# The inversion of the gated-DeltaNet blocks: 16x16 blocks by row substitution on VectorE, with the blocks copied to the lanes through DRAM, in place of three levels of block doubling on TensorE

## The reference

```python
kb = kc * bc[..., None]
a = jnp.where(strict, jnp.einsum('nbhid,nbhjd->nbhij', kb, kc) * decay, 0.0)
ia = a + jnp.eye(lc, dtype=jnp.float32)
u = lax.linalg.triangular_solve(ia, vc * bc[..., None], left_side=True, lower=True, unit_diagonal=True)
w = lax.linalg.triangular_solve(ia, kb * jnp.exp(gcum)[..., None], left_side=True, lower=True, unit_diagonal=True)
```

## Time and profile before

| what | us |
|---|---|
| median of 3 runs | 1892.87 |
| lowest, highest | 1892.07, 1893.97 |
| profiled execution, span | 1893.0 |
| PE busy | 1867.0 |
| DVE busy | 1087.0 |
| ACT busy | 729.3 |
| POOL busy | 223.4 |

### The profile page before, as it was taken

How to read it: one execution, slowest core, us unless ns; L and a number is a source line. 1 busy time by engine, 2 the same in 40 slices (tenths; PEclk the granted TensorE clock), 3 DMA queues, 4 the chain that set the end, 5 groups by cost and what they waited for, 6 DMA issues and landing times.

```text
span 1893.0 us, 31005 instructions
## 1 busy us (share of the span) xinstructions
PE 1867.0 (99%) x9409; PEld 1579.4 (83%) x9409; DVE 1087.0 (57%) x2433; ACT 729.3 (39%) x1467; POOL 223.4 (12%) x379
## 2 busy tenths in 40 slices
PE   7999999999999999999999999999999999999997
PEld 6999998888888888888888888888888888888886
DVE  6666666888888874564545454433334444444455
ACT  4444444545444433353333333333333333333330
POOL 2343432222222200001110110000000000000000
PEclk9999999999999999999999999999999999999999
DMA  8666665444444435346555646544444555456541
GB/s 216 168 166 162 161 171 126 109 113 111 114 110 113 116 120 161 94 128 163 157 158 161 172 122 170 162 129 128 129 130 142 150 161 161 127 166 211 162 134 67
DMA packets 317412, 270.76 MB, mean 143 GB/s; under 512 B 96600, under 2 KB 230624, under 8 KB 316704
## 3 DMA queue, kind: packets, MB, share of 16 engines
q1 hardware_dynamic: 306880, 250.90, 47.3%
q0 software_dynamic: 10464, 18.99, 4.1%
HBM read 249.73 MB, written 20.06 MB: 143 GB/s over the span
## 4 chain that ended last, share of the span: by engine, by line
PE 98%; DVE 1%; DMA 0%; issue 0%; SPq 0%; ACT 0%; DVEq 0%; POOL 0%; ACTq 0%; POOLq 0%
PE bank L296 71%; PE bank L2013 9%; PE bank L1749 7%; PE bank L1865 2%; PE bank L1242 1%; PE bank L1224 1%; PE bank L1236 1%; PE bank L1218 1%; PE bank L415 0%; DMA x_res<-in_x_sample 0%; PE bank L638 0%; PE bank L1192 0%; PE bank L1285 0%; PE bank L1214 0%; PE bank L1200 0%
## 5 line engine op out<-in xcount | busy, mean ns | idle before, releaser
L272 DVE TENSOR_TENSOR w_lo<-raw,w_hi 128x512 fp32r<-128x512 f32 (+2 forms) x828 | 562.4, 688 | 620.9 <-ACT w_hi L267 616.8
L267 ACT ACTIVATE w_hi<-raw 128x512 fp32r<-128x512 f32 (+2 forms) x828 | 502.4, 616 | 838.6 <-PE bank L296 703.1
L296 PE MATMUL bank<-w_hi,aT_hi 128*128 128x512 f32 (+2 forms) x1776 | 696.3, 392 | 1.7 <-DVE aT_lo L430 1.6
L296 PE MATMUL bank<-w_hi,aT_lo 128*128 128x512 f32 (+2 forms) x1776 | 673.6, 379 | 0.0
L296 PE MATMUL bank<-w_lo,aT_hi 128*128 128x512 f32 (+2 forms) x1776 | 672.6, 379 | 0.0
L296 PEld LDWEIGHTS bank<-w_hi,aT_hi 128*128 128x128 f32 x1776 | 334.8, 189 | 58.7 <-issue 9.7
L296 PEld LDWEIGHTS bank<-w_hi,aT_lo 128*128 128x128 f32 x1776 | 334.0, 188 | 55.7
L296 PEld LDWEIGHTS bank<-w_lo,aT_hi 128*128 128x128 f32 x1776 | 335.1, 189 | 47.7
L296 PE MATMUL bank<-w_hi,hT_hi 128*128 128x512 f32 x288 | 112.1, 389 | 0.0
L296 PE MATMUL bank<-w_lo,hT_hi 128*128 128x512 f32 x288 | 112.1, 389 | 0.0
L296 PE MATMUL bank<-w_hi,hT_lo 128*128 128x512 f32 x288 | 112.0, 389 | 0.0
(11 more groups left out here) (365 smaller groups left out, 1962.5 us busy)
## 6 DMA issues: line engine op xcount, KB each, us to landing
raw<-in_ffn_w_gate SPq DMA_DIRECT2D x176, 256.0 KB, 2.7
raw<-in_ffn_w_up SPq DMA_DIRECT2D x176, 256.0 KB, 2.7
raw<-in_ffn_w_down SPq DMA_DIRECT2D x176, 256.0 KB, 3.4
raw<-in_w_in SPq DMA_DIRECT2D x128, 192.0 KB, 2.4
raw<-in_w_in SPq DMA_DIRECT2D x128, 128.0 KB, 2.3
raw<-in_w_in SPq DMA_DIRECT2D x256, 64.0 KB, 2.3
raw<-in_w_out SPq DMA_DIRECT2D x61, 256.0 KB, 3.3
h_blocks<-sg SPq DMA_DIRECT2D x11, 768.0 KB, 4.6
```

What stands on the lines that cost most here:

```text
L267: nc.scalar.activation(w_hi[:, g % RING, 0:width], raw[:, g % RAW, 0:width], ACT.Copy).then_inc(sem("w_high"), 1)
L272: nc.vector.tensor_tensor(w_lo[:, g % RING, 0:width], raw[:, g % RAW, 0:width], w_hi[:, g % RING, 0:width], ALU.subtract).then_inc(sem("w_ ...
L296: last = nc.tensor.matmul(acc[t][:, 0:width], l[:, k0 + n, t * P:(t + 1) * P], r[:, g % RING, 0:width], start=(n == 0 and j == 0), stop=(n ...
```

## The change

Levels 1, 2 and 3 go from PE and DVE. The inverse of each 16x16 block on the diagonal is computed instead by DVE, one row of the block in each lane (partition): from k = 15 down to 1, column k of the inverse so far times row k of the block is subtracted. For that, each lane needs the whole 16x16 block of its own group of 16 lanes, for all three tiles (768 numbers, 3 KB). SP moves them: 8 stores (one for each group, 16 lanes x 3 tiles x 16 numbers, pieces of 64 bytes) to DRAM, a wait until all have landed, and 8 loads, each of one DRAM row of 3 KB to 16 lanes, into the storage of U and Z, which are one tile now. The move stands in SP's order ahead of load 15 (`LOW_AT`), behind load 14. The row steps are in DVE's slots 19, 22 and 25 (`ROWS_AT`), 5 values of k in each, 2 operations for a k, each followed by `after`. Then T is made from the blocks by a mask, and U from it by transposes as before. Levels 4, 5, 6 move from slots 27, 31, 34 to 28, 32, 35. The value's convolution moves to slots 9 (tap 0) and 14 (taps 1, 2), the rough root to slot 17. The masks of the levels 0 to 3 go from the constants, two smaller ones come.

```diff
+ROWS_AT = (19, 22, 25)
+ROWS_OF = (range(BLOCK - 1, 10, -1), range(10, 5, -1), range(5, 0, -1))
+LOW_AT = NP_IN - 1
+LEVEL_AT = {4: 28, 5: 32, 6: 35}
...
+                A = early[:, 0:TOK].rearrange("p (t c) -> p t c", t=TT)
+                inv, prod = (early[:, TOK + n * TT * BLOCK:TOK + (n + 1) * TT * BLOCK]
+                             .rearrange("p (t c) -> p t c", t=TT) for n in range(2))
...
+                UZ = sb(ctx, "UZ", [P, 2, TT, P])
+                U, Z = UZ[:, 0], UZ[:, 1]
+                low = UZ[:].rearrange("p a t c -> p (a t c)")
+                below = low.rearrange("p (t k c) -> p t k c", t=TT, k=BLOCK)
+                low_blocks = nc.dram_tensor("low_blocks", (GROUPS, TT * BLOCK * BLOCK), F32, kind="Internal").ap()
...
-                    for n in range(1, LEVELS):
+                    for n in range(LOW, LEVELS):
+                        step = n - LOW + 1
                         yield LEVEL_AT[n]
...
-                    after(ins)
-                    after(V.tensor_tensor(B, A, lv[0].unsqueeze(1).broadcast_to([P, TT, P]), ALU.mult))
-                    V.tensor_tensor(T[:], ident.unsqueeze(1).broadcast_to([P, TT, P]), B, ALU.subtract)\
-                        .then_inc(sem("g_T1"), 1)
+                    ins.then_inc(sem("g_A"), 1)
+                    V.tensor_copy(inv, cn[:, C_OWN:C_OWN + BLOCK].unsqueeze(1).broadcast_to([P, TT, BLOCK]))
+                    conv(2, range(1))
+                    yield 14
+                    conv(2, range(1, TAP - 1))
+                    yield 17
+                    rsqrt_rough(nrs[:], nss[:, 1, :], npol[:], after)
+                    for at, ks in zip(ROWS_AT, ROWS_OF):
+                        yield at
+                        dve.wait_ge(sem("g_low_in"), 16 * GROUPS * (h + 1))
+                        for k in ks:
+                            after(V.tensor_tensor(prod[:, :, 0:k], below[:, :, k, 0:k],
+                                                  inv[:, :, k:k + 1].broadcast_to([P, TT, k]), ALU.mult))
+                            after(V.tensor_tensor(inv[:, :, 0:k], inv[:, :, 0:k], prod[:, :, 0:k], ALU.subtract))
+                    V.tensor_tensor(T[:].rearrange("p t (g c) -> p t g c", g=GROUPS),
+                                    inv.unsqueeze(2).broadcast_to([P, TT, GROUPS, BLOCK]),
+                                    cn[:, C_SAME:C_SAME + P].rearrange("p (g c) -> p g c", g=GROUPS).unsqueeze(1)
+                                    .broadcast_to([P, TT, GROUPS, BLOCK]), ALU.mult).then_inc(sem("g_T1"), 1)
                     W("g_T1")
                     V.transpose(U[:, 0, :], T[:, 0, :]).then_inc(sem("g_Ua"), 1)
                     V.transpose(U[:, 1:3, :], T[:, 1:3, :]).then_inc(sem("g_Ub"), 1)
...
-                        if n in (1, 2, 3):
-                            conv(2, range(n - 1, n))
-                        if n == 3:
-                            rsqrt_rough(nrs[:], nss[:, 1, :], npol[:], after)
...
+                def move_low(eng, h):
+
+                    eng.wait_ge(sem("g_A"), h + 1)
+                    for g in range(GROUPS):
+                        own = slice(g * BLOCK, (g + 1) * BLOCK)
+                        eng.dma_start(low_blocks[g].rearrange("(t k c) -> k t c", t=TT, k=BLOCK), A[own, :, own])\
+                            .then_inc(sem("g_low_out"), 16)
+                    eng.wait_ge(sem("g_low_out"), 16 * GROUPS * (h + 1))
+                    for g in range(GROUPS):
+                        eng.dma_start(low[g * BLOCK:(g + 1) * BLOCK, :], low_blocks[g].partition_broadcast(BLOCK))\
+                            .then_inc(sem("g_low_in"), 16)
...
                         for n in range(NP_IN):
                             next_state(sp, n, i)
+                            if n == LOW_AT:
+                                move_low(sp, i + 1)
                             loads(sp, G_GDN + 2 * NP_IN + n + NP_IN * i, n % RAW, gdn_parts(i + 2, n, n % RAW))
```

More of the change, by code:

```diff
@@ L101 @@
 C_LV = C_MS + 2 * P
+LOW = 4
 LEVELS = 7
+BLOCK = 1 << LOW
+GROUPS = P // BLOCK
 SQUARE = 32
-SAMPLE_LEVELS = 4
 F_OWN = 14
@@ L139, in constants @@
     c[:, C_MS + P:C_MS + 2 * P] = np.where((col <= row) & same, 0, NEG)
[L140 to L143, removed]
+    for n in range(STEPS):
+        s = 1 << LOW + n
+        above = (row // (2 * s) == col // (2 * s)) & (row // s % 2 == 0) & (col // s % 2 == 1)
+        c[:, C_LV + n * P:C_LV + (n + 1) * P] = above
+    c[:, C_SAME:C_SAME + P] = row // BLOCK == col // BLOCK
+    c[:, C_OWN:C_OWN + BLOCK] = row % BLOCK == col[:, 0:BLOCK]
     c[:, C_BM:C_BM + NB] = row // NQ == np.arange(NB)[None, :]
@@ L1152, in encoder_layer @@
                 cvb = (b4, b5, b3)
-                lv = [cn[:, C_LV + n * P:C_LV + (n + 1) * P] for n in range(LEVELS)]
-                def n_tiles(level):
-                    return TT if (1 << level) < NQ else 2
+                lv = {LOW + n: cn[:, C_LV + n * P:C_LV + (n + 1) * P] for n in range(STEPS)}
                 def tl(x, t, c=P):
@@ L1221, in gdn_pe @@
                             nc.tensor.transpose(tl(b5, 1), U[:, 0, :], ident).then_inc(sem("g_Ta_ps"), 1)
[L1222 to L1225, removed]
+                        L("g_Ub", step, STEPS + 1)
+                        nc.tensor.matmul(tl(b6, 1), A[:, 1, :], U[:, 1, :], start=True, stop=True)\
+                            .then_inc(sem("g_Zb_ps"), 1)
                         if 1 << n > SQUARE:
-                            for t in range(1, n_tiles(n)):
-                                last = nc.tensor.transpose(b7[:, (t - 1) * P:t * P], U[:, t, :], ident)
-                            last.then_inc(sem("g_Tb_ps"), 1)
+                            nc.tensor.transpose(b7[:, 0:P], U[:, 1, :], ident).then_inc(sem("g_Tb_ps"), 1)
                         yield LEVEL_AT[n] + 1
-                        L("g_Za", n, LEVELS - 1)
-                        if n > 1:
-                            L("g_Ta", n - 1, LEVELS - 2)
+                        L("g_Za", step, STEPS)
+                        if step > 1:
+                            L("g_Ta", step - 1, STEPS - 1)
                         else:
@@ L1237, in gdn_pe @@
                             .then_inc(sem("g_UZa_ps"), 1)
[L1238 to L1243, removed]
+                        L("g_Zb", step, STEPS)
+                        if step > 1:
+                            L("g_Tb", step - 1, STEPS - 1)
+                        nc.tensor.matmul(tl(b7, 2), T[:, 1, :], Z[:, 1, :], start=True, stop=True)\
+                            .then_inc(sem("g_UZb_ps"), 1)
                         if n == 4:
@@ L1455, in gdn_dve @@
                     V.transpose(U[:, 1:3, :], T[:, 1:3, :]).then_inc(sem("g_Ub"), 1)
[L1456 to L1459, removed]
+                    for n in range(LOW, LEVELS):
+                        step = n - LOW + 1
+                        yield LEVEL_AT[n]
+                        L("g_Za_ps", step, STEPS)
                         V.tensor_tensor(Z[:, 0, :], tl(b4, 0), lv[n], ALU.mult).then_inc(sem("g_Za"), 1)
[L1461 to L1464, removed]
+                        L("g_Zb_ps", step, STEPS)
+                        V.tensor_tensor(Z[:, 1, :], tl(b6, 1), lv[n], ALU.mult).then_inc(sem("g_Zb"), 1)
                         if n == 4:
@@ L1636, in gdn_sp @@
                     for n in range(RAW + A_DVE, NP_IN):
+                        if n == LOW_AT:
+                            move_low(sp, 0)
                         loads(sp, G_GDN + NP_IN + n, n % RAW, gdn_parts(1, n, n % RAW))
@@ L1643, in gdn_sp @@
                         next_state(sp, n, HEADS - 2)
+                        if n == LOW_AT:
+                            move_low(sp, HEADS - 1)
                         if n == OUT_STORE_AT:
```

38 lines of the change are left out of this document (18 added, 20 removed).

## The result

The changed kernel took 1991.8 us (median of 4 runs, 1989.9 to 1993.5) against 1893.1 us (1892.1 to 1894.0): ratio 1.052, 95% interval 1.051 to 1.054. 98.7 us were lost; 92 were forecast.

What follows compares the result with a forecast made beforehand. PE, busy in 99% of the span, was taken to bound the kernel. Stands 8.8, level 6 0.7 and clock 2.0 made 11.5 us per head, +92 us over 8 heads: 1893 to 1985 us, range 1935 to 2028.

Steps and rivals of the forecast that it cites:

- PE's saving: Levels 1 to 3 leave PE: 18 products per head, 4.3 us saved per head, 34.5 us over 8 heads.
- The order on SP: Load 14, then stores and loads issued 0.46 us apart, landing in 2.2 and 2.4; DVE waits from 523.0 to 532.0.
- The row steps: 30 chained small operations on DVE, about 0.20 us each plus some 0.03 for size: batches of 2.3, 2.15, 2.0 us.
- PE's two stands: PE stands for piece 9, then for U before level 4; 8.8 us lost per head, PE's saving already inside.
- Level 6: One slot nearer its reader, so PE waits 0.7 us per head for U; bounds 0 and 0.9.
- The clock: PE restarts at 1.2 GHz after its stand, slowing level 4 and later work: 2.0 us per head, bounds 0 and 3.2.
- Rival 4: PE's clock stays up or returns at once: 9.5 us per head, 1969 us; chance 0.81 together with the forecast.
- Sum: 8.8 + 0.7 + 2.0 = 11.5 us per head, +92 us over 8 heads, 1985 us.
- fewer constants: Smaller constants, seen only as one load at the start: hidden, at no cost or gain.
- 1 (transfers hidden): Transfers hidden, DVE's rows alone set U: +0.5 us per head, 1897 us; chance 0.06.
- 2 (faster): Blocks there by 519.85, row steps under 0.1 us, PE keeps all 4.3 us per head: 1858 us; chance 0.05.
- 3 (dear issues): SP's 16 new issues cost 0.55 us more each, 8.8 us more per head: 2055 us; chance 0.08.

Runs made afterwards that it cites:

- e8: Changed kernel with level 6 one slot earlier (slot 34 instead of 35): 1990.9 us.
- e5b: Changed kernel with 31 unused products on PE at slot 26 and 19 more ahead of level 4, filling both stands: 1978.1 us.
- e9: Changed kernel with a 368-column gap, the move ahead of load 14, row steps together behind piece 9's split, level 4 at slot 29, level 6 at 34: 1950.6 us.
- e10: e9 with 34 unused 128x128 products on PE ahead of level 4: 1940.3 us.
- e1: Changed kernel with an unused tile of 368 columns behind the constants, putting later tiles back where they lay before the change: 1980.3 us.
- e3: Changed kernel without the stores, loads and DVE's wait; row steps read constants, so the inversion's values are wrong: 1931.4 us.
- e4: Changed kernel with the move and DVE's wait but without the 30 row steps, so values are wrong: 1939.6 us.
- e6: Changed kernel with the move one place earlier in SP's order, ahead of load 14: 1981.1 us.
- e2: Kernel before the change with an unused tile of 16 columns (64 bytes per lane) behind the constants: 1906.0 us.
- e2b: Kernel before the change with an unused tile of 32 columns (128 bytes per lane) behind the constants: 1905.2 us.
- e5: Changed kernel with 31 unused 128x128 products on PE at slot 26, filling the first stand only: 1994.9 us.
- e7: Changed kernel with the move ahead of load 14, DVE gathering each lane's numbers, one store and one load replacing 8 and 8, and a 368-column gap: 1957.6 us.

## Why the prediction was right

**PE's saving** was forecast at 4.3 us per head. It can be read where the levels 1 to 3 are done before and PE does not yet stand after, at the last matmul of piece 8, here before and after:
```profile
530.17 0.39 PE L296 MATMUL bank<-w_hi,aT_lo 128*128 128x512 f32 x1
```
```profile
566.72 0.39 PE L306 MATMUL bank<-w_hi,aT_lo 128*128 128x512 f32 x1
```
That is 25.2 us into the head (from 504.95) and 21.2 (from 545.51): 4.0 us saved.

**The order on SP** was right: load 14 first, stores 0.46 us apart, all landed before the first load. The landings were 2.2 (stores) and 2.0 (loads), against 2.2 and 2.4. SP begins the stores 15.9 us into the head as forecast. The last store landed 1.6 us after its issue began and the last load 1.9, where I had counted 2.2 and 2.4. DVE had the blocks 25.9 us into the head; forecast 27.0 (531.9 - 504.95). DVE's wait was 7.2 us instead of 9.0: 1.1 of it by this, the rest because DVE reached it later (its taps, roots and splits end 18.6 us into the head, forecast 18.0).

The Trainium skill, "DMA: Bandwidth & Descriptors", section "Anatomy of one DMA — SWDGE (gpsimd) path", has about 2 us of fixed cost for a transfer issued by GpSimd; the small transfers here, issued by SP, agree with it (2.2 and 2.0). It would not have given the 4.6 to 6.4 us of the single 384 KB load: with the term for bytes in that section my estimate is 2.9.

**The row steps** were sized right: five pairs of 45 to 33 elements from 571.40 to 573.7, 2.3 us (forecast 2.3), the next ten steps 2.2 (2.15), the last ten 2.0 (2.0). From start to start a step of 45 elements took 0.24 us and one of 3 elements 0.20; the rows of before, 0.20 for 3 elements, were enough.

**PE's two stands**: forecast 8.8 us, then 3 to 4 for U. Measured 7.5 and 2.8. Level 4 starts 34.8 us into the head shown, and 34.7 to 35.0 in the six heads beside the input projection, against 27.0 for the same point of before: 7.8 us lost where 8.8 were forecast. This is the mis-sized term, by -1.0 us per head, and it is the transfers' (above).

**Level 6**: forecast 0.7, measured 0.7 (5.8 us over 8 heads). The size was right, the reading of it too simple: e8 shows that it isn't bound to the slot of level 6.

**The clock**: forecast 2.0 us per head. From the start of level 4 to that of level 6 before took 8.6 us (531.26 to 539.90 in the earlier trace rows); after took 11.6 in the head shown, and 10.1 to 11.6 in the eight heads, 10.6 on the mean: a loss of 2.0. In e5b all of it is gone, and 0.3 of it is lost again on the filler. Behind the one stand of e9 the clock costs less, 1.3 (e10). Rival 4, no loss by the clock, falls. That the sum had just 2.0 is in part luck: it was picked between bounds of 0 and 3.2. The earlier trace rows was a fair place for the upper one: its records start 0.21 us apart until 18.6 us and 0.11 from there. The Trainium skill, "TensorE: Matmul & The Clock Gate", section "HAM oscillation — how this bites in real kernels", tells of matmuls that lose their clock at every wait for a DMA; every one of the 8 heads here did, though the wait that PE itself saw was one for DVE.

**Sum**: 7.8 + 0.7 + 2.0 = 10.5 us per head; the seven periods give 10.6. 8 x 10.6 = 85. Forecast 92. Another 11.5 us come from the placement of tiles (e1), a step that the prediction didn't have: I had put "fewer constants" down at nothing and named only their load. Two errors of opposite sign thus made the total look better than its parts: that 98.7 lies so near to 92 is luck. 85 + 11.5 is 96 to 97 of 98.7. The spans of the two profiled executions differ by 95.3 us (1988.3 - 1893.0), and there it adds up: eight heads 85, the work behind them 12.8, and up to A of the first head after is 2.4 us ahead of before, which I have not taken apart.

**Rivals.** 1 (transfers hidden): DVE waits 57.7 us for them. 2 (faster) needed the blocks 14.9 us into the head and row steps under 0.1 us; they came at 25.9, and a step took 0.20 to 0.24. With either part made free by itself (e3, e4) the kernel is still slower than before; both free at once was not run. 3 (dear issues): 0.42 us each. None of the versions that I ran comes below 1931 us, and none that computes the whole inversion below 1940.

## What to carry to other kernels

Work that leaves the engine in the chain is worth its time only if the work that replaces it is ready when that engine asks for it: here 4.0 us were taken from PE, and the time from A to the input of level 4 went from 13.0 us (518.2 to 531.3) to 21.5 (558.8 to 580.3). Look at what is queued behind the waiting instruction: PE's longest stand is put down to a split of unrelated weights that stood behind DVE's wait. With the splits out of the way and level 4 one slot later (e9) about 18 us were won, with the transfers started earlier (e6) 10.7; but most of the stand, 8.7 us, stays as long as the blocks come so late. And when a change makes any tile smaller, compare the records of untouched stages before and after, for the tiles behind it have moved.

## What the runs showed of the hardware

- **Placement.** The same matmuls with hT as moving operand take 389 or 395 to 396 ns each by where the tiles behind the constants lie in the partition, displaced by 64 or 128 bytes; over this kernel 11 to 13 us (e1, e2, e2b). Why, the runs don't show.
- **The clock falls in short stands.** In e3 and e5, with one stand of 4.1 us in each head, the granted clock went to 0.50 in every head, as it did with stands of 5.3 (e4), 7.5 and 2.8 (after) and 8.7 us (e9). With what the filler left of the stands, 1.4 us at most, it stayed at 1.00 (e5b, e10). In after, in the head shown, it was at 0.50 for 17 us, 11 of them before level 4. A stand isn't the only occasion: in before it was at 0.50 from 63.0 to 69.8 us, where PE's records have no gap, behind products of 128x8 (L717, 24 records).
- **One big spread load was no faster than eight small ones.** 384 KB over 128 lanes in one load landed in 4.6 to 6.4 us (e7, with loads of weights beside it); eight loads of 48 KB over 16 lanes took 5.1 from the first issue, 2.0 each (after). Small stores landed in 2.9 us issued 0.7 us behind a load of 512 KB (e6) and in 2.2 issued 3.2 us behind it (after); that the load is the cause is not shown.
